# Feature-major products with the streamed operand read, and the output written, from the last column to the first

## What is computed

```python
h = h + 0.5 * swiglu(rmsnorm(h), w_gate, w_up, w_down)      # 1024 -> 2816 -> 1024
u = rmsnorm(h)
q, k, v, r, lr, z, xbc, dt, aq, ak, av, gates = u @ w_in    # split by columns
h = h + (g0 * (o_gla @ w_gla) + g1 * (y_ssm @ w_ssm) + g2 * (o_att @ w_att)) @ w_out
h = h + 0.5 * swiglu(rmsnorm(h), w_gate2, w_up2, w_down2)
out = rmsnorm(h)
```

## Time and profile before

| | |
|---|---|
| median of three runs | 1799.5 us |
| span of the profiled execution | 1798.7 us |
| TensorE matmuls busy | 1786.7 us (99%), 10012 instructions |
| TensorE weight loads busy | 1506.3 us (84%) |
| VectorE busy | 958.3 us (53%) |
| ScalarE busy | 632.9 us (35%) |
| GpSimd busy | 90.8 us (5%) |
| mean granted TensorE clock | 0.998 of full |

### The profile page before, as it was taken

One profiled execution on the slowest core, in us unless ns is written; L12 is line 12 of the kernel. 1 busy time (PEld: TensorE's weight loads), 2 busy tenths in 40 slices (PEclk: granted clock), 3 DMA queues, 4 the chain that ended last, 5 costly groups with the idle time before them and its releaser, 6 DMA issues.

```text
span 1798.7 us, 26473 instructions
## 1 busy us (share of the span) xinstructions
PE 1786.7 (99%) x10012; PEld 1506.3 (84%) x10012; DVE 958.3 (53%) x1385; ACT 632.9 (35%) x1002; POOL 90.8 (5%) x92
## 2 busy tenths in 40 slices
PE   9999999999999999999999999999999999999998
PEld 7888888888788888888988888888888888888887
DVE  5444443379888888622544446654334544444333
ACT  5322322244444454332333334443222323222221
POOL 2111100000000000000000000000000011111000
PEclk9999999999999999999999999999999999999999
DMA  5323223333233332223222222222222322223332
GB/s 171 105 93 100 98 94 105 106 99 90 83 82 93 87 86 84 82 95 103 94 71 71 93 82 93 90 84 73 102 95 94 103 90 99 93 94 103 106 105 72
DMA packets 53938, 169.30 MB, mean 94 GB/s; under 512 B 6337, under 2 KB 13761, under 8 KB 53873
## 3 DMA queue, kind: packets, MB, share of 16 engines
q1 hardware_dynamic: 45824, 159.15, 27.1%
q10 hardware_dynamic: 8048, 9.24, 2.6%
HBM read 166.21 MB, written 2.16 MB: 94 GB/s over the span
## 4 chain that ended last, share of the span: by engine, by line
PE 97%; DVE 2%; DMA 0%; ACT 0%; issue 0%; POOL 0%; SPq 0%; DVEq 0%; ACTq 0%; POOLq 0%
PE G L546 50%; PE I L546 16%; PE G L613 12%; PE G L566 8%; PE I L1040 1%; PE I L1016 1%; PE I L1006 1%; PE G L868 1%; PE I L673 1%; PE I L808 1%; PE I L817 1%; PE I L827 1%; PE I L794 0%; PE I L976 0%; PE I L980 0%; PE I L778 0%
## 5 line engine op out<-in xcount | busy, mean ns | idle before, releaser
L1657 DVE TENSOR_TENSOR WL<-RAW,WH 128x1024 fp32r<-128x1024 f32 x296 | 372.0, 1260 | 288.7 <-ACT WH L1137 279.4
L1137 ACT CAST WH<-RAW 128x1024 fp32r<-128x1024 f32 x295 | 307.1, 1046 | 223.3 <-PE I L546 126.4
L546 PE MATMUL G<-UH,WH 128*128 128x512 f32 x664 | 164.3, 389 | 0.0
L546 PE MATMUL G<-UL,WH 128*128 128x512 f32 x664 | 164.0, 389 | 0.0
L546 PE MATMUL G<-UH,WL 128*128 128x512 f32 x664 | 164.0, 389 | 0.0
L546 PEld LDWEIGHTS G<-UL,WH 128*128 128x128 f32 x664 | 124.6, 188 | 25.9
L546 PEld LDWEIGHTS G<-UH,WL 128*128 128x128 f32 x664 | 124.6, 188 | 25.9
L546 PEld LDWEIGHTS G<-UH,WH 128*128 128x128 f32 x664 | 124.5, 188 | 25.8
L546 PE MATMUL G<-NH,WH 128*128 128x512 f32 x448 | 114.8, 398 | 0.3 <-ACTq L1291 0.3
L546 PE MATMUL G<-NL,WH 128*128 128x512 f32 x448 | 110.7, 389 | 0.0
L546 PE MATMUL G<-NH,WL 128*128 128x512 f32 x448 | 110.7, 389 | 0.0
(11 more groups left out here) (351 smaller groups left out, 2622.3 us busy)
## 6 DMA issues: line engine op xcount, KB each, us to landing
RAW<-in_slabs SPq DMA_DIRECT2D x296, 512.0 KB, 3.4
cum_rows<-kept_rows ACTq DMA_DIRECT2D x16, 256.0 KB, 6.8
bias<-in_rel ACTq DMA_DIRECT2D x16, 128.0 KB, 2.8
bias<-in_rel ACTq DMA_DIRECT2D x16, 112.0 KB, 2.6
h<-in_x SPq DMA_DIRECT2D x6, 256.0 KB, 6.4
out_y<-h SPq DMA_DIRECT2D x4, 256.0 KB, 2.2
h<-in_x ACTq DMA_DIRECT2D x2, 256.0 KB, 3.5
out_y<-h ACTq DMA_DIRECT2D x4, 128.0 KB, 1.8
```

Source lines behind the costliest of these rows:

```text
L546: ins = mm(dst, slab(W, n)[:, (k - k0) * P:(k - k0 + 1) * P], R[:, k, :], start=begin and which == 0 and k == k0, stop=end and which == 2 ...
L1137: nc.scalar.copy(slab(WH, n), RAW[:, n.slot, :]).then_inc(split_hi, 1)
L1657: V.tensor_tensor(slab(WL, n), RAW[:, n.slot, :], slab(WH, n).bitcast(F32), ALU.subtract).then_inc(split_lo, 1)
```

## The change

A helper `mm_back` reverses the last axis of both the output and the streamed operand of a matmul, and every feature-major matmul goes through it. The stationary operand is read as before; `weights` is only a shorter way to write the same slice. Column c of the output is still the product of column c of the streamed operand, so what is computed is the same. No wait, no increment, no order, no address range and no token-major, transpose or chunk product is changed.

```diff
+        def weights(W, n, b):
+            return slab(W, n)[:, b * P:(b + 1) * P]
...
+            def mm_back(dst, stationary, streamed, start, stop):
+                return mm(dst[:, ::-1], stationary, streamed[:, ::-1], start=start, stop=stop)
...
-                        ins = mm(dst, slab(W, n)[:, (k - k0) * P:(k - k0 + 1) * P], R[:, k, :],
+                        ins = mm_back(dst, weights(W, n, k - k0), R[:, k, :],
```

More of the change, by code:

```diff
@@ L565, in fm_piece @@
                 for k in range(k0, k0 + 4):
-                    ins = mm(dst, slab(W, n)[:, k * P:(k + 1) * P], R[:, k, :], start=piece == 0 and k == 0,
+                    ins = mm_back(dst, weights(W, n, k), R[:, k, :], start=piece == 0 and k == 0,
                              stop=piece == 5 and k == KT - 1)
@@ L578, in fm_fresh @@
                     pe.wait_ge(hi_ready, 8 * stage + k + 1)
-                    mm(dst, slab(WH, n)[:, k * P:(k + 1) * P], RH[:, k, :], start=k == 0, stop=False)
-                    mm(dst, slab(WL, n)[:, k * P:(k + 1) * P], RH[:, k, :], start=False, stop=False)
+                    mm_back(dst, weights(WH, n, k), RH[:, k, :], start=k == 0, stop=False)
+                    mm_back(dst, weights(WL, n, k), RH[:, k, :], start=False, stop=False)
                     pe.wait_ge(lo_ready, 8 * stage + k + 1)
-                    ins = mm(dst, slab(WH, n)[:, k * P:(k + 1) * P], RL[:, k, :], start=False, stop=k == KT - 1)
+                    ins = mm_back(dst, weights(WH, n, k), RL[:, k, :], start=False, stop=k == KT - 1)
                 ins.then_inc(slab_done, 1)
@@ L592, in fm_first @@
                     pe.wait_ge(uh_ready, k + 1)
-                    mm(dst, slab(WH, n)[:, k * P:(k + 1) * P], UH[:, k, :], start=k == 0, stop=False)
+                    mm_back(dst, weights(WH, n, k), UH[:, k, :], start=k == 0, stop=False)
                     if k == 0:
@@ L597, in fm_first @@
                         need_slab(n)
-                    mm(dst, slab(WL, n)[:, k * P:(k + 1) * P], UH[:, k, :], start=False, stop=False)
+                    mm_back(dst, weights(WL, n, k), UH[:, k, :], start=False, stop=False)
                     pe.wait_ge(ul_ready, k + 1)
-                    ins = mm(dst, slab(WH, n)[:, k * P:(k + 1) * P], UL[:, k, :], start=False, stop=k == KT - 1)
+                    ins = mm_back(dst, weights(WH, n, k), UL[:, k, :], start=False, stop=k == KT - 1)
                 ins.then_inc(slab_done, 1)
@@ L672, in last_half @@
                     for k in range(k0, k1):
-                        ins = mm(dst, slab(W, n)[:, (k - k0) * P:(k - k0 + 1) * P], R[:, k, HALVES[half_no]],
+                        ins = mm_back(dst, weights(W, n, k - k0), R[:, k, HALVES[half_no]],
                                  start=(c, which) == (0, 0) and k == 0, stop=(c, which) == (2, 2) and k == k1 - 1)
@@ L867, in output_part @@
                         b = block0 + k - k0
-                        ins = mm(G[:, wn.slot, :], slab(W, n)[:, b * P:(b + 1) * P], R[:, k, :],
+                        ins = mm_back(G[:, wn.slot, :], weights(W, n, b), R[:, k, :],
                                  start=begin and which == 0 and k == k0, stop=end and which == 2 and k == k1 - 1)
```

## The result

The changed kernel takes 1832.6 us (median of three runs, 1830.2 to 1832.6), 33.1 us more than before: a ratio of 1.0179, 95% interval 1.0160 to 1.0197. The forecast of no change was wrong. Of the cases named, the time falls in that of the unsettled pattern (1820 to 1835 us), but the trace shows that its mechanism isn't what happened.

A forecast was written before the change was run, and what follows sets the result against it. TensorE's matmul distances were taken to bound the kernel. Nothing was added and the edit was put at zero, so 1798.7 + 0 us in the profiled execution, 1799.5 us as median; range 1757 to 1838 us.

The forecast's parts named there:

- The forecast of no change: Whole kernel: the settled matmul distance stays at 226.7 ns, time 1799.5 us, own range 1796 to 1803 us; chance 0.34.
- the unsettled pattern: Dense feature-major stretches: opposed reads never lock, +3.3 to +5.8 ns per matmul, 1820 to 1835 us; chance 0.23.
- What bounds the kernel: TensorE, busy 1786.7 of 1798.7 us: time is a sum of matmul distances, each gain or loss reaching the end nearly whole.
- The count and the price of a nanosecond: All feature-major matmuls: 6138 on the path that sets the end, so one nanosecond in each is 6.14 us, 0.34%.
- I take zero for the edit, because the row nearest to it is the settled 226.7 itself: Feature-major matmuls: 226.7 ns, the same for every tensor, bank and width, may hold for reversed order; change 0 us.
- The prediction's own last sign: Feature-major matmuls: prediction most wrong if the fixed step of 16 ticks is an accident of the forward direction.
- The bound above, 36 us: All 6138 feature-major matmuls at the first four's start-up distance, 232.5 ns: +5.8 ns each, +36 us, 1835 us.
- The better pattern: Feature-major matmuls: reversed reads meet elsewhere, excess settles at about half, 2.2 to 6.7 ns gained, 1786 to 1758 us; chance 0.23.
- The sign named for these matmuls: 256-column feature-major matmuls: move by the 512-column ones' nanoseconds if excess belongs to the weight load, half if to columns.
- Not at full rate: Feature-major matmuls: backward access takes a 1.2 GHz tick per column, +203 ns each, about 3046 us; chance 0.13.
- The token-major stretch should stay at 11.3 us in all cases: Token-major stretch of 96 matmuls: stays at 11.3 us; if it moves, each matmul's excess isn't its own access's.
- The inference of two reads in each other's way: Feature-major matmuls: streamed read and next weight load interfere at full rate, settling in a pattern that costs 16 ticks, 13.3 ns.

The follow-up runs named there:

- read_back: Changed kernel with the output written forward again; feature-major matmuls still read the streamed operand backward: 1831.6 us, ratio 1.0177.
- write_back: Changed kernel with the streamed operand read forward again; only the output is written backward: 1799.7 us, ratio 1.0006.
- tm_48: Kernel before, all forward, token-major slabs meant to stand 48 elements later; by a slip tensors behind the ring buffers moved by 32: 1818.2 us, ratio 1.0105.
- micro_a: No layer computed: stretches of 72 matmuls alone, varying direction, operand shift and columns; 512 columns without shift: 226.7 ns forward, 233.3 backward.
- tail_back: Kernel before, all forward except the last 8 feature-major matmuls ahead of token-major slab pairs at 16 places: 1795.9 us, ratio 0.9978.
- micro_e: No layer computed: 48-matmul stretches with narrower stationary blocks, other lengths, or one 500 to 508 column matmul ahead; 512 columns after these: 226.7 ns forward, 233.3 backward.
- micro_b: No layer computed: 48-matmul stretches with streamed, output or stationary columns walked in other orders, and token-major stretches after different matmuls; orders with chunks reversed: 226.7 to 233.3 ns.

## Why the prediction was wrong, point by point

- **What bounds the kernel: right.** Span, TensorE's busy time and the sum of matmul distances moved together, and every nanosecond in a matmul reached the end.
- **The count and the price of a nanosecond: right.** 6138 matmuls, 6.14 us for each nanosecond. The mean distance of the 512-column ones in dense stretches, with the unsettled starts, went from 227.0 to 233.4 ns: 6.37 x 6006 = +38.3 us. The 132 of 256 columns gave back 1.4 x 132 = 0.2 us, token-major 5.9 us ( 233.32 to 227.45). The sum is +32.2 us, the growth of the span.
- **"I take zero for the edit, because the row nearest to it is the settled 226.7 itself": the step that failed.** The edit costs 6.7 ns for each matmul of 512 columns, and the streamed read alone does it (read_back 233.3, write_back 226.7). The zero rested on 226.7 being the same for every tensor and bank. By the kernel's layout all of them stand at one place modulo 64 elements, and moving one changes its value (tm_48). micro_a shows that value as the exception, kept only forward at a shift of 0 (or 64), and 228.8 to 233.3 at the others. The other support was that the excess is 13.3 ns at 256 columns as at 512. That doesn't show a fixed step: forward it is 11.7 to 16.5 ns at other lengths, and backward it grows from 11.7 to 20.0. The prediction's own last sign, a step that is an accident of the forward direction, is what came. A trace in which every case has one alignment can't show how much hangs on it; that the token-major rows, with another alignment, differed was the warning, and I gave it 2.2 ns and the wrong sign.
- **The unsettled rival: right side and nearly the time, wrong mechanism.** Priced at 230.0 to 232.5 ns from the start-up; what came is a settled 233.3 that backward streams reach within a few matmuls of a rest, and after every entry. That the time fell in this rival's range is luck. The bound above, 36 us, fell short of the steady part, 40 us, and only the token-major gain brought the time under it.
- **The better pattern: wrong at 512 columns, right at 256** (118.3 ns alone, for 120.0), of which the kernel has 132. The sign named for these matmuls, the same nanoseconds as at 512 or half as many, came as neither: -1.4 ns against +6.7.
- **Not at full rate: out.** No row of after is near 427 ns at the full clock, and the backward write costs nothing.
- **"The token-major stretch should stay at 11.3 us in all cases": wrong**, by its own test. Each matmul's distance is not its own access's alone: stretches with several settled patterns take one by what ran before (tail_back, micro_e).
- **The inference of two reads in each other's way: half shown.** Shown: the relative place of the two operands matters, with nothing beside, and so does the order in which the stationary block is read (233.3 to 245.0 ns, micro_b); at half clock neither direction costs. Refuted: that the excess is made by the amount that the load reads. What mechanism gives 20.0 ns backward stays open.

## What to carry to other kernels

In a kernel bound by dense matmuls with new stationary blocks, measure the distance from start to start and its excess over one column per tick, and vary the place of the streamed operand against the stationary one and the order of its groups before you touch anything else: here that was worth -3% to +18% of a matmul at 512 columns, without the strides that break groups of 4 or hit the period. In the kernel itself the best order tried gained 0.5%. A value that all tensors share may only mean that they share an alignment. Measure an order after several entries: one stretch can settle in a pattern that the kernel doesn't reach, as 220.0 ns did.

## What the runs showed of the hardware that I had not expected

- The direction in which PSUM is written is free (write_back 1.0006), as is an output in chunks of 4 at a step of 16; the direction of the streamed read costs 6.7 ns per 512 columns at 2.4 GHz and nothing at 1.2 GHz (427 ns apart either way).
- The forward distance has a period of 64 float32 elements in the relative place of the operands: 226.7, 228.9, 232.4 and 233.3 ns at 0, 16, 32 and 48.
- Many settled distances are multiples of 6.67 ns, 8 ticks of 1.2 GHz: 113.3, 120.0, 146.7, 206.7, 220.0, 226.7, 233.3, 240.0, 266.7; but 118.3, 223.3, 230.0 and 236.7 ns are not, so it is no rule.
- One order of access can settle at different distances, 220.0 or 230.7 ns, depending on a few columns in a single matmul before it.
